# Order of the products in a recurrence-and-window mixer on one Trainium2 core

## What is computed

```python
proj = h @ w_in                                   # 1024 x 1792
xb, gate, q, k, v = split(proj, [512, 1024, 1536, 1664])
# recurrence half
xc = causal_depthwise_conv_2(xb, conv_w) + conv_b
r  = sigmoid(blockdiag(w_a) @ xc + b_a)
gi = sigmoid(blockdiag(w_i) @ xc + b_i)
log_a = -8 * r * softplus(-lam);  a = exp(log_a)
u  = sqrt(-expm1(2 * log_a)) * (gi * xc)
y_lru = scan(a, u) * gelu(gate)                   # h[t] = a[t] h[t-1] + u[t]
# attention half: 8 query heads, 2 key and value heads of width 64
q, k = rope(rms_norm(q)), rope(rms_norm(k))
y_att = sliding_window_attention(q, k, v, sinks)  # window 128
out = concat([y_lru, y_att]) @ w_out
```

## Time and profile before

| | us |
|---|---|
| median of 3 runs | 2855.66 (2854.65 to 2855.91) |
| the profiled execution, its own time | 2853.37 |
| its span in the trace | 2851.5 |
| third mixer: first input product (PE) to last addition (DVE) | 1204.56 to 1332.27 |
| of it, attention: first scores (PE) to last scaling (DVE) | 1261.94 to 1299.22 |

### The profile page before, as it was taken

How to read it: one execution, slowest core, us unless ns; L and a number is a source line. 1 busy time by engine, 2 the same in 40 slices (tenths; PEclk the granted TensorE clock), 3 DMA queues, 4 the chain that set the end, 5 groups by cost and what they waited for, 6 DMA issues and landing times. The chain is left out here.

```text
span 2851.5 us, 37838 instructions
## 1 busy us (share of the span) xinstructions
PE 2584.1 (91%) x14166; PEld 2179.8 (76%) x14166; DVE 1834.5 (64%) x2413; ACT 1419.0 (50%) x1875; POOL 366.9 (13%) x255
## 2 busy tenths in 40 slices
PE   7778978998998799888998997689999999999998
PEld 6447846997987499765997977578888888888886
DVE  3654354546665454464545734488888888888886
ACT  4131124445553243333434621167777777777776
POOL 3102120003443000000002432100000000000000
PEclk9889898998998899987999989889999999999999
DMA  6610022544421255521554300189999999999995
GB/s 239 190 46 14 1 89 98 193 166 150 148 89 60 79 177 193 174 89 45 193 193 175 131 18 1 72 324 375 377 370 383 362 384 371 367 383 367 380 368 219
DMA packets 180082, 574.02 MB, mean 201 GB/s; under 512 B 10958, under 2 KB 80718, under 8 KB 136844
## 3 DMA queue, kind: packets, MB, share of 16 engines
q1 hardware_dynamic: 175884, 558.01, 53.1%
q0 software_dynamic: 3120, 11.27, 1.6%
q10 hardware_dynamic: 976, 3.33, 0.3%
HBM read 564.46 MB, written 6.29 MB: 200 GB/s over the span
## 5 line engine op out<-in xcount | busy, mean ns | idle before, releaser
L2921 DVE TENSOR_TENSOR moe_weights_low<-ring,moe_weights_high 128x1024 fp32r<-128x1024 f32 x672 | 782.3, 1218 | 103.6 <-ACT moe_weights_high L3158 101.0
L3158 ACT CAST moe_weights_high<-ring 128x1024 fp32r<-128x1024 f32 x672 | 686.5, 1053 | 109.3 <-PE banks L256 106.0
L254 PE MATMUL banks<-moe_weights_high,moe_rows_high 128*128 128x512 f32 x896 | 354.5, 396 | 3.1 <-DVE moe_rows_low L2926 2.5
L256 PE MATMUL banks<-moe_weights_low,moe_rows_high 128*128 128x512 f32 x896 | 350.3, 391 | 0.0
L255 PE MATMUL banks<-moe_weights_high,moe_rows_low 128*128 128x512 f32 x896 | 349.5, 390 | 0.0
L254 PE MATMUL banks<-ffn_x_high,ffn_weights_high 128*128 128x256 f32 x1056 | 301.3, 285 | 8.4 <-DVE ffn_x_low L441 8.4
L255 PE MATMUL banks<-ffn_x_high,ring_low 128*128 128x256 f32 x1056 | 300.4, 284 | 0.0
L256 PE MATMUL banks<-ffn_x_low,ffn_weights_high 128*128 128x256 f32 x1056 | 300.1, 284 | 0.0
L2732 DVE TENSOR_TENSOR ring_low<-ring,ffn_weights_high 128x2048 fp32r<-128x2048 f32 x60 | 134.8, 2288 | 133.9 <-ACT ffn_weights_high L2706 133.9
L254 PEld LDWEIGHTS banks<-ffn_x_high,ffn_weights_high 128*128 128x128 f32 x1056 | 202.2, 191 | 12.3 <-DVE ffn_x_low L441 9.6
L255 PEld LDWEIGHTS banks<-ffn_x_high,ring_low 128*128 128x128 f32 x1056 | 202.5, 192 | 2.6
(11 more groups left out here) (570 smaller groups left out, 5040.2 us busy)
## 6 DMA issues: line engine op xcount, KB each, us to landing
ring<-in_moe_gate_pieces SPq DMA_DIRECT2D x112, 1024.0 KB, 7.2
ring<-in_moe_up_pieces SPq DMA_DIRECT2D x112, 1024.0 KB, 7.4
ring<-in_moe_down_pieces SPq DMA_DIRECT2D x112, 1024.0 KB, 7.3
ring<-in_ffn_w SPq DMA_DIRECT2D x66, 1024.0 KB, 7.7
ring<-in_od_w_in SPq DMA_DIRECT2D x10, 2048.0 KB, 8.1
ring<-in_o_w_in SPq DMA_DIRECT2D x8, 2048.0 KB, 8.3
ring<-in_e_ffn_w_gate SPq DMA_DIRECT2D x11, 1024.0 KB, 5.4
ring<-in_e_ffn_w_up SPq DMA_DIRECT2D x11, 1024.0 KB, 8.0
```

Of the source, the lines that this page charges most:

```text
L254: pe.matmul(out_, lh, rh, start=start, stop=False)
L256: return pe.matmul(out_, lh, rl, start=False, stop=stop)
L2921: dve.tensor_tensor(lo[:, b], piece, hi[:, b].bitcast(F32), ALU.subtract).then_inc(sems["lo_done"], 1)
L3158: act.copy(hi[:, b * 1024:(b + 1) * 1024], piece).then_inc(sems["hi_done"], 1)
```

## The change

The order of the calls in `lru_and_window` becomes: the recurrence's input product with convolution; the first 512 columns of queries, keys and values, with the small block products between its two token tiles (`recurrence_gates`); the last 256 columns; on DVE then `decay_rates`, the heads of tile 0 (`turn_heads(0)`), `one_less`, the heads of tile 1; the gate's product; `square_root` and `inputs`; the attention, which has only `gated_scan` left in its list, in round 1. No arithmetic is added or taken away.

```diff
-            project(xT, KD, a["e_w_in_2"][0], (H + 2 * KVH) * N, normed, copy_out(qkv), first_col=2 * LW)
-            qkv_have = both()
...
-            for t in range(TT):
-                head_norm(view[t][:, 0:H, :], H, N, [qkv_have, V.at()], gq, scratch[:, 0:H, :])
...
             conv_project(a["e_w_in_2"][0], 0, NT4, taps, bias, params_landed, normed, ACT.Identity, finish)
             x_ready = S.at()
+            r, gi = room3(NT4, T), room3(NT4, T)
+
+            def recurrence_gates():
+                for i in range(NT4):
+                    bank = take_bank()
+
+                    @block.tensor
+                    def _(pe):
+                        for due in unseen(pe, bank.free, x_ready):
+                            pe.wait_ge(*due)
+                        for due in unseen(pe, par_blocks.landed()):
+                            pe.wait_ge(*due)
+                        pe.matmul(bank.ap[:, 0:T], blocks_a[:, i, :], x[:, i, :], start=True, stop=True)
+                        pe.matmul(bank.ap[:, T:2 * T], blocks_i[:, i, :], x[:, i, :], start=True, stop=True).then_inc(*M.tick())
+                    have = M.at()
...
+            qkv_cols, made = (H + 2 * KVH) * N, {}
+
+            def take_first(ps, mark, t, c0, n):
+                free = copy_out(qkv)(ps, mark, t, c0, n)
+                if t == 0:
+                    made["squashed"] = recurrence_gates()
+                return free
+            project(xT, KD, a["e_w_in_2"][0], 512, normed, take_first, first_col=2 * LW)
+            project(xT, KD, a["e_w_in_2"][0], qkv_cols - 512, normed,
+                    lambda ps, mark, t, c0, n: copy_out(qkv)(ps, mark, t, c0 + 512, n), first_col=2 * LW + 512)
+            qkv_have = both()
...
-            project_turned(a["e_w_in_2"][0], LW, NT4, normed, take)
-            gate_ready = S.at()
-            r, gi = room3(NT4, T), room3(NT4, T)
-            for i in range(NT4):
-                bank = take_bank()
...
+            def turn_heads(t):
+                head_norm(view[t][:, 0:H, :], H, N, [qkv_have, V.at()], gq, scratch[:, 0:H, :])
+                done = head_norm(view[t][:, H:HK, :], KVH, N, V.at(), gk, scratch[:, 0:KVH, :])
...
+            decay_rates()
+            turn_heads(0)
+            one_less()
+            rotated = turn_heads(1)
+            project_turned(a["e_w_in_2"][0], LW, NT4, normed, take)
+            gate_ready = S.at()
+            square_root()
+            inputs()
             have = paired_attention(qkv, H, KVH, N, N ** -0.5, lambda i: y[:, :, i * N:(i + 1) * N], rotated,
-                                    const("band"), sinks, [decay_rates, one_less, square_root, inputs, gated_scan])
+                                    const("band"), sinks, [lambda: None, gated_scan])
```

More of the change, by code:

```diff
@@ L3326, in lru_and_window, with _ @@
             x_ready = S.at()
+            r, gi = room3(NT4, T), room3(NT4, T)
[11 more added lines that the diff above has]
+                    have = M.at()
+                    @block.scalar
+                    def _(act):
+                        act.wait_ge(*have)
+                        act.activation(r[:, i, :], bank.ap[:, 0:T], ACT.Sigmoid, bias=b_a[:, i:i + 1]).then_inc(*S.tick())
+                        act.activation(gi[:, i, :], bank.ap[:, T:2 * T], ACT.Sigmoid, bias=b_i[:, i:i + 1]).then_inc(*S.tick())
+                    bank.free = S.at()
+                return S.at()
+            qkv_cols, made = (H + 2 * KVH) * N, {}
[8 more added lines that the diff above has]
+            qkv_have = both()
             def take(i, ps, mark):
@@ L3333, in take @@
                 return S.at()
-            project_turned(a["e_w_in_2"][0], LW, NT4, normed, take)
-            gate_ready = S.at()
-            r, gi = room3(NT4, T), room3(NT4, T)
-            for i in range(NT4):
-                bank = take_bank()
[L3340 to L3350, removed]
-                    for due in unseen(act, qkv_have):
-                        act.wait_ge(*due)
-                    act.wait_ge(*have)
-                    act.activation(r[:, i, :], bank.ap[:, 0:T], ACT.Sigmoid, bias=b_a[:, i:i + 1]).then_inc(*S.tick())
-                    act.activation(gi[:, i, :], bank.ap[:, T:2 * T], ACT.Sigmoid, bias=b_i[:, i:i + 1]).then_inc(*S.tick())
-                bank.free = S.at()
-            squashed = S.at()
+            HK = H + KVH
+            scratch = room(HK * N).rearrange("p (n m) -> p n m", m=N)
+            halves = [room(HK * 32).rearrange("p (n m) -> p n m", m=32) for _ in range(2)]
+            view = [qkv[:, t, :].rearrange("p (n m) -> p n m", m=N) for t in range(TT)]
+            def turn_heads(t):
+                head_norm(view[t][:, 0:H, :], H, N, [qkv_have, V.at()], gq, scratch[:, 0:H, :])
+                done = head_norm(view[t][:, H:HK, :], KVH, N, V.at(), gk, scratch[:, 0:KVH, :])
+                cos, sin = (const(n).rearrange("p (t m) -> p t m", t=TT)[:, t, :].unsqueeze(1).to_broadcast([P, HK, 32])
+                            for n in ("rope_cos", "rope_sin"))
+                return rotate(view[t][:, 0:HK, 0:32], view[t][:, 0:HK, 32:64], cos, sin, None, done, halves)
+            squashed = made["squashed"]
             root = room3(NT4, T)
-            made = {}
             def decay_rates():
```

8 lines of the change are left out of this document (removed).

## The result

The median of the changed kernel is 2861.13 us (13 runs, 2859.70 to 2863.15), that of the kernel before, on the same chips, 2854.06 (13 runs). The ratio is 1.0024, 95% interval 1.0017 to 1.0032 (4.9 to 9.1 us): **7.1 us slower**. The forecast was +7.6 on a base of 2855.66, which turned out 1.6 above the median of more runs; hence 2863.3 instead of some 2861.7.

A forecast was written before the change was run, and what follows sets the result against it. The bound was taken to move between PE (input products) and DVE (heads, attention). First scores 14.8 us later, less 7.2 us of shorter attention, gave +7.6 on 2855.66, so 2863.3 us; range 2857.0 to 2866.5.

The forecast's parts named there:

- What bounds the kernel before: Third mixer, 130 us: bound moves from PE in input products to DVE in heads, then a hole, then DVE in attention.
- the hole of 7.35 us: DVE idle before attention, up to 1261.08, waiting for ACT's sigmoids, small products and convolution; claimed to go whole.
- Input products: PE: queries, keys and values end 17.4 us later; convolution hidden under products, sigmoids on idle ACT; first heads operation at 1243.35.
- DVE in order: DVE from 1243.35: decay_rates, heads 0, one_less, heads 1, square_root, durations added up, ending at 1274.65.
- ACT's wait: ACT's square root ahead of key and query copies holds first scores on DVE to 1278.85, 14.8 us later than before.
- The attention's length: Attention shortens by 7.2 us with fillers gone, ending at 1306.7 to 1306.8 against 1299.22: +7.6 us.
- the 11.8 us of fillers: Recurrence steps on DVE leaving the attention; 7.2 us of length given back, the rest had covered waits.
- The cancelling parts: Before the attention: heads' start 17.4 us later, less 7.35 us hole and 8.0 us convolution, +2.0 us if nothing else changed.
- Rival A: PE's clock rises in the attention: +0.6 to +2.6 us, or +5.0 if only the last values halve; chance 0.25.
- Rival B: Attention gets no shorter, waits take every gap a filler leaves: +14.8 us, 2870.5; chance 0.07.
- Rival C: Faster: hole and convolution count fully, or root's wait shorter, plus higher clock: -1.6 us, 2854.1; chance 0.08 including anything unseen.

The follow-up runs named there:

- e3_root_after_copies: Changed kernel with ACT's square root behind the copies of keys and first queries, and inputs in round 1 ahead of gated_scan: 2861.58 us, ratio 1.0023.
- e2_root_back: Changed kernel with square_root and inputs back in the attention's rounds 0 and 1, gated_scan in round 2: 2858.60 us, ratio 1.0015.
- e4_gate_five_times: Changed kernel with the products of the gate's last tile made five times over, same result, to keep PE busy: 2861.61 us, ratio 1.0027.
- e5: Changed kernel with decay_rates, one_less and square_root among the input products, inputs and gated_scan in the attention's rounds 0 and 1: 2859.44 us, ratio 1.0017.
- e1: Changed kernel with only the new order of input products; all recurrence steps returned to the attention's list as before the change: 2858.10 us, ratio 1.0014.
- e6_conv_between_heads: Kernel before the change with one move, DVE's convolution between the heads of tile 0 and tile 1: 2850.91 us, ratio 0.9990.
- e8_half_early: Changed kernel with decay_rates and one_less among the input products; square_root, inputs and gated_scan in the attention's list: 2854.87 us, ratio 1.0001.
- e7_small_in_gate: Kernel before the change with convolution between the two tiles' heads and small products with sigmoids behind the gate's second tile: 2851.04 us, ratio 0.9989.
- e11: Repeat of e5 without an edit, for a second profile: 2858.36 us, ratio 1.0015 against the kernel before.

## Why the prediction was right

By its own steps, with the 2.86 us of the later start taken off the rows of after:

- **What bounds the kernel before.** One reading was off: the hole of 7.35 us is put down to sigmoids that wait for the small products. The products were made from 1254.28 on, but the first sigmoid started at 1258.01, for ACT had two table loads of 1.28 us and the gate's four GELUs (1.21 us) ahead of it. Some 3.8 us of the hole are ACT's own order. The sum does not hang on it, since the whole hole goes either way.

```profile
1254.28 0.67 PE L3345 MATMUL banks<-arena 128*128 128x256 f32 x2 [1.18 <-DVE arena L1889]
...
1258.01 0.48 ACT L3354 ACTIVATE arena<-banks,small_tensors 128x256 f32<-128x256 f32 x1
```

- **Input products.** Right. The first operation of decay_rates came at 1243.12 (1245.98 - 2.86), forecast 1243.35. The convolution was done under its products and some 2 us more (DVE's idle 15.09 us begin at 1223.64, the products end at 1221.50), the sigmoids fell on an idle ACT.
- **DVE in order.** Heads 0 at 1245.52 (1245.65), one_less 1255.29 (1255.5), heads 1 1259.41 (1259.5), square_root 1269.16 (1269.3). DVE works from 1243 on without a gap but those inside the heads, which their 9.9 us contain, so adding durations was good to 0.3 us.
- **ACT's wait.** Root at 1274.54 (1274.7), keys' copy at 1275.50 (1275.66), scores on DVE at 1278.61 (1278.85). That it is the root which holds them up e3_root_after_copies and e2_root_back showed: with the root behind the copies they come 4.2 us earlier.
- **The attention's length.** 27.6 us from first scores to last scaling instead of 34.9: 7.2 us given back, as forecast, of the 11.8 us of fillers. Why the rest did not come back, the chain through ACT and PE, shows in DVE's idle time between first scores and last scaling: 4.1 us before (34.87 less 30.81 busy), 8.0 us after (27.64 less 19.69), of it 1.32 us for the last scores and 1.91 us for the first scaling of the last pair. The 0.99 us in front of each of the last scalings were there before as well. Attention end 1306.54, forecast 1306.75. Behind it all is shifted alike: SP's first issue after the mixer is 9.94 us later in the profile of after (2.86 + 7.1), its last one 9.60.
- **The cancelling parts.** "+2.0 us, if nothing else changed" was too low as a price for the order of products: alone it costs 3.7 us in the median and 4.2 at the first scores. The sum did not rest on it, but the text left out that the chain which turns the keys had been hidden by convolution and hole; exposed, it adds 2.86 - 0.71 = 2.15 us, just the difference. In after this term is covered by square_root and the root's wait.
- **Rival A (the clock rises).** Fell. PE was busy for 9.49 of the 10 us from 1293 on at 0.50, and the clock rose only in the output product, at 1315; the second profile of after shows the same 0.50. e4_gate_five_times shows that it does not hang on the long idle stretch either. It was not far off, though: in e5, whose attention holds the same work, the clock did return twice, and that gave 0.5 us. It did not return in the last values, whose halving rival A counts at 2.6 us. The rule of the Trainium skill, TensorE: Matmul & The Clock Gate, section Why this matters for your kernels, that unbroken work brings the full clock, held for the 128x512 products; the 5.22 us of values from 1303.78 on, without a gap and at 0.50, did not bear it out.
- **Rival B (+14.8).** Fell: 7.2 us came back. Perfetto Trace Analysis of the Trainium skill, section Optimization Strategy, advises interleaving regimes; e1 and e2 show that it depends on what the filler hides: square_root in the wait for the turned keys is free, while one_less and square_root in rounds 1 and 2 cost 6.5 of their 9.3 us.
- **Rival C (faster).** Fell for this change. A gain was to be had by another order, e6_conv_between_heads.

## What to carry to other kernels

When a step is moved into an idle stretch, first find which chain the work around it had been hiding (here POOL, PE and ACT turning the keys), since that chain becomes the next wait; a filler is free only up to its length. To close a hole in one engine, try first to reorder that engine's own queue: here moving the convolution between two groups of heads gained 3.4 us, while moving PE's products to the same end lost 3.7 alone and 7.1 with the steps put ahead of the attention. Spread the fillers of an attention over its rounds: inputs and gated_scan in one round made it 1.6 us longer than one in each of two rounds. Where a stage's end is set by one engine without gaps, sums of durations from the trace were good to 0.3 us; count them from a common row, because the start of the stage differed by up to 2.9 us between profiles, nearly as much as the best gain.

## What the hardware showed beyond that

The return of the full clock behind the attention is not fixed to the work. Turning and output product are the same in all kernels, yet from the last scaling to the last addition they took 32.2 to 33.9 us, and the later the clock rose, the longer: 32.2 us with the rise 5.9 us after the start of the last scaling (e1_products_only, 0.68 in the slice from 1310), 32.6 us after 6.7 (before), 33.9 us after 9.2 (e8_half_early, 0.51 in the slice from 1306). That is 1.7 us, half of what the best reordering gained, and it took away 1.2 us from e8_half_early and 0.7 from e7_small_in_gate. It fits half the clock for 3.2 us more. What decides the moment was not tried.

POOL's two copies of the keys took 0.73 us with DVE at a reciprocal beside them (e3_root_after_copies) and 2.06 us with DVE at an elementwise product of two tensors in SBUF (e5 and e11). So a DVE step that is moved next to POOL's work may lengthen a chain through POOL; that the product is the cause was not tested by itself.
